# The first row of tokens turned ahead of the last projection quarter, and the next stage's first products of that row begun early

## The chip, the cores and the metric

The kernel runs on one core of one Trainium2 chip. Its engines are TensorE (PE; its weight loads, which overlap the products, are shown as PEld), VectorE (DVE), ScalarE (ACT), GpSimd (POOL) and SyncE (SP), which issues the transfers. The metric is the device time of one execution in microseconds (us).

## The reference

A sequence of 256 tokens of width 1024 goes through two blocks. The first has an attention layer with two kinds of heads (causal attention and differential attention) and a feed-forward layer that chooses 16 of 16384 experts for each of 8 heads. The second has two more attention layers, mixer A (three dilated groups) and mixer B (a neighbourhood on a grid). Everything is float32. Cut to what matters here:

```python
h = rms_norm(x, attn_norm); proj = h @ w_in          # attention of block 1 on proj
x = x + mixed @ w_out                                # the output projection
h = rms_norm(x, ffn_norm)                            # peer_ffn
q = (h @ w_query).reshape(C, 8, 2, 128)              # the first thing it computes
sc = einsum('thpd,hpnd->thpn', q, sub_keys)          # top 16, experts, gelu, sum
x = x + peer_out
hn = rms_norm(x, norm_gain[0]); x = x + mixer_a(hn)  # ends in y @ w_out, too
hn = rms_norm(x, norm_gain[1]); x = x + mixer_b(hn)  # starts with hn @ w_in
```

At each `rms_norm` all 1024 values of a token's x must be there, and the product behind it needs the normed tokens with the width on the partitions: they are turned (transposed) by TensorE.

## The kernel before, in words

x lies in on-chip memory as two rows of 128 tokens (`NT` = 2), each 1024 wide. The width is also cut into `KD` = 8 steps of 128, over which TensorE sums a product.

`attention_phase` runs three times: `block1` (named `block` in the trace), `mix_a` and `mix_b`. Each has one instruction list per engine, written in order: an engine works its list in order and waits at semaphores. A phase is a `Block`, at whose end all engines meet; the next phase starts on all of them together. Its pairs of heads go through a written schedule (`times_of`, `due`, `step`): products of the normed tokens with a weight piece into the banks `pj[0]` and `pj[1]`, eviction, norm of queries and keys, their turn (`turn_qk`), scores, softmax, turn, product with the values (`ot`), turn of the output (`yp`).

The output projection has four quarters b: row b // 2 of tokens, half b % 2 of the width, eight steps k each (`project`, line 720). Their banks are `acc`: `pj[0]`, `pj[1]`, `xp` and the first half of `sc`. A few of these steps are set between the last attention steps (`in_tail`); the others follow at the end in the order of `at_end`, line 503: first quarter 0, last quarter 3. In `block1` seven steps of quarter 3 are left at the end, k = 1 to 7; in `mix_a` all eight. A float32 product of this kind is two instructions in the trace.

Then comes the norm for the next phase (where `after` is given: `block1` and `mix_a`). VectorE adds a quarter to x (`add`); ScalarE squares a row and sums it; VectorE makes the root and scales the row (`next_scaled`, line 1098); TensorE turns it in eight transposes into two banks (line 775; row 0 into `pt` and the second half of `sc`, row 1 into `pj`); VectorE writes each half times the gain into `whole` (`next_window`, line 1104); ScalarE copies it, rounded, into `hT` high, and VectorE writes the rest into `hT` low (`next_low`, line 1110). In the lists before the change TensorE turns both rows after all four quarters, VectorE makes row 0's windows after the last addition and its low parts after the second row is scaled, and ScalarE squares both rows before it copies. Fillers (`keep_clock`, line 218: products with the unit matrix that nobody reads) stand between the two turns, behind the second, and at the start of `mix_b`; `WARM` has their numbers.

After `block1` the routing stage starts (`route_phase`). SP issues four loads of `route_raw` in the order 2, 3, 0, 1, then the first loads of the early chunks (each behind one of the first two query products), then reloads. TensorE makes 16 query products. The first two are plain, `down_raw` with `whole` over all 256 tokens (line 1422; their weights were loaded in the phase before). From the third on the weight is split: ScalarE writes the high part (line 1458), GpSimd the low part (line 1409), and TensorE makes three passes (lines 210 to 212). Behind each query product but the first stand the scores of the query before (line 1439), which also need that query's `route_raw`.

`mix_b` starts with the split of its first weight piece, `mix_raw` (ScalarE line 802, VectorE line 582), in four parts; the product of row 0 and that of row 1 run in three passes of 384 columns for each step, then the gate product in three passes of 256 (its weight, transferred from the start of the phase, is split at lines 881 and 1045), then the first product of the next pair, and behind its first part the turn of the first pair's queries and keys (line 667), which needs their norm from VectorE (lines 902 to 919).

Of the kernel before, what the change touches and what calls it, by code (L numbers as in the profile page):

```python
# [30 lines left out]
P = 128  # L31
# [37 lines left out]
WARM = {"open": 8, "row": 14, "last": 8, "experts": 10, "added": 10, "rows": (11, 6), "mix_b": 6}  # L69
# [245 lines left out]
def attention_phase(nc, name, pieces, *, n_pairs, kinds, groups, hT, yT, cons, q_gain=None, k_gain=None,  # L315
                    bias=None, load_bias=None, near=None, minus_lam=None, ahead=None, behind=None, finish=None, x, wo, wo_landed, fills, beside=None, lead=None, after=None, out=None):
# [88 lines left out]
    with ExitStack() as c:  # L405
# [48 lines left out]
        pj = [ps(f"pj{b}", [P, 512]) for b in range(2)]  # L454
# [3 lines left out]
        ot = ps("ot", [P, 2, SEQ])  # L458
        yp_bank = ps("yp", [P, 512])
# [37 lines left out]
        def pj_of(par, i):  # L497
            return (nch * par + i) % 2
# [8 lines left out]
        def _(sp):  # L507
# [20 lines left out]
            def one(q, qb):  # L528
# [6 lines left out]
                if ring == 1:  # L535
                    load_piece(q + 2, qb, 0)
# [59 lines left out]
        def _(pe):  # L596
# [10 lines left out]
            def product(q, qb, i, part):  # L607

                dst, j = pj[pj_of(qb, i)], piece_of[i]
                if lead is not None and isinstance(q, int) and q == 0 and i == NT and part == 0:  # L610
                    pe.wait_ge(first_low, 2 * NT)
# [40 lines left out]
                if part == cut - 1:  # L652
                    mm.then_inc(products, 1)

# [131 lines left out]
        def _(act):  # L786
# [103 lines left out]
            if after is not None:  # L890
# [3 lines left out]
                for n in range(2 * NT):  # L894
                    act.wait_ge(next_full, n + 1)
# [1107 lines left out]
```

## Time and profile before

| | us |
|---|---|
| median of 3 runs | 1597.7 |
| lowest, highest | 1596.82, 1598.11 |
| the profiled execution | 1597.93 |
| its span, from the first to the last instruction | 1596.2 |
| TensorE busy | 1549.2 |
| VectorE busy | 1012.3 |
| ScalarE busy | 690.8 |

A line of a timeline has the start in us from the span's start, the duration in us, the engine, the line of the kernel, the operation, what it writes and reads, its shape and how many like it were merged; in square brackets the time that the engine had been idle before it and who released it. "SPq" is the queue of transfers that SP issues. A line of a windows view has the stretch, its length, the busy time and number of instructions of each engine, the granted clock of TensorE (1.00 is 2.4 GHz), the share of time that the DMA engines were busy, and GB/s.

### The profile page before, as it was taken

The page shows a single profiled execution, that of the slowest core. Times are in us where ns is not written, and L with a number is a line of the kernel's source. Part 1 is how long each engine was busy: PE and PEld are TensorE (multiplying, and loading weights), DVE is VectorE, ACT ScalarE, POOL GpSimd, SP SyncE. Part 2 cuts the span into 40 slices and gives each one's busy share as a digit, 9 for nine tenths or more (in the row PEclk, how much of TensorE's full clock was granted, in tenths as well). Part 3 has the DMA queues.
Part 4 walks back from the last instruction along what each step waited for, and adds up shares of the span by engine and source line. Part 5 has one row for each costly group of instructions (what it writes and reads, how often), then busy time and mean ns, then how long its engine had stood idle before and what let it go on. Part 6 is the DMA issues. An engine that isn't in the chain of part 4 may idle for free. (4 is left out here: it accounts for less than half of the span.)

```text
span 1596.2 us, 29115 instructions
## 1 busy us (share of the span) xinstructions
PE 1549.2 (97%) x9001; PEld 1351.8 (85%) x9001; DVE 1012.3 (63%) x2525; ACT 690.8 (43%) x1537; POOL 42.0 (3%) x42
## 2 busy tenths in 40 slices
PE   7998999999999999999999999999999999899998
PEld 4664698888888888999999999979999999669994
DVE  4666589967776776666666666665555555247762
ACT  2433241222223444444444444435666655336661
POOL 0000160000000000000000000000000000000000
PEclk9999999999999999999999999999999999999999
DMA  7410344433225555655555555547544443317530
GB/s 285 169 56 1 119 145 144 152 100 93 93 80 197 191 191 178 204 184 184 186 186 190 186 189 189 186 161 230 178 146 146 145 147 120 116 30 230 160 110 27
DMA packets 163803, 240.40 MB, mean 151 GB/s; under 512 B 41744, under 2 KB 91408, under 8 KB 162192
## 3 DMA queue, kind: packets, MB, share of 16 engines
q1 hardware_dynamic: 163728, 239.46, 46.5%
q8 instruction: 39, 0.64, 0.2%
q14 instruction: 36, 0.29, 0.1%
HBM read 238.14 MB, written 1.29 MB: 150 GB/s over the span
## 5 line engine op out<-in xcount | busy, mean ns | idle before, releaser
L210 PE MATMUL experts_acc<-experts_uh,experts_wh 128*128 128x512 f32 x512 | 200.3, 391 | 0.4 <-DVE experts_ul L1787 0.4
L211 PE MATMUL experts_acc<-experts_ul,experts_wh 128*128 128x512 f32 x512 | 200.1, 391 | 0.0
L212 PE MATMUL experts_acc<-experts_uh,experts_wl 128*128 128x512 f32 x512 | 199.2, 389 | 0.0
L1257 PE MATMUL plain_u<-whole,down_raw 128*128 128x256 f32 x832 | 190.6, 380 | 0.7 <-PEq L1342 0.4
L1757 ACT ACTIVATE experts_uh<-whole 128x512 fp32r<-128x512 f32 x256 | 147.0, 623 | 81.0 <-PE experts_acc L212 75.4
L212 PE MATMUL projection<-hT_high,down_low 128*128 128x256 f32 x608 | 172.1, 283 | 0.0
L211 PE MATMUL projection<-hT_low,down_high 128*128 128x256 f32 x608 | 172.0, 283 | 0.0
L210 PE MATMUL projection<-hT_high,down_high 128*128 128x256 f32 x608 | 171.7, 282 | 0.0
L1257 PEld LDWEIGHTS plain_u<-whole,down_raw 128*128 128x128 f32 x832 | 152.5, 190 | 20.1 <-issue 1.7
L1787 DVE TENSOR_TENSOR experts_ul<-whole,experts_uh 128x512 fp32r<-128x512 f32 x256 | 164.7, 684 | 0.0
L210 PE MATMUL mix_a_pj<-mix_a_wh,hT_high 128*128 128x384 f32 x368 | 129.1, 351 | 0.0
L212 PE MATMUL mix_a_pj<-mix_a_wh,hT_low 128*128 128x384 f32 x368 | 123.5, 336 | 0.0
L211 PE MATMUL mix_a_pj<-mix_a_wl,hT_high 128*128 128x384 f32 x368 | 123.5, 336 | 0.0
L1793 DVE TENSOR_TENSOR experts_full<-experts_full,spread 128x256 f32<-128x256 f32 x76 | 32.3, 425 | 141.3 <-ACT experts_full L1322 141.3
L210 PEld LDWEIGHTS projection<-hT_high,down_high 128*128 128x128 f32 x608 | 116.4, 191 | 2.9
L211 PEld LDWEIGHTS projection<-hT_low,down_high 128*128 128x128 f32 x608 | 116.4, 191 | 2.9
L212 PEld LDWEIGHTS projection<-hT_high,down_low 128*128 128x128 f32 x608 | 116.4, 191 | 0.0
L1298 ACT ACTIVATE down_high<-down_raw 128x512 fp32r<-128x512 f32 x152 | 95.3, 632 | 46.5 <-DMA down_raw<-in_downT 41.3
L212 PEld LDWEIGHTS experts_acc<-experts_uh,experts_wl 128*128 128x128 f32 x512 | 96.2, 188 | 20.5
L210 PEld LDWEIGHTS experts_acc<-experts_uh,experts_wh 128*128 128x128 f32 x512 | 96.4, 188 | 18.8 <-issue 0.8
L211 PEld LDWEIGHTS experts_acc<-experts_ul,experts_wh 128*128 128x128 f32 x512 | 96.4, 188 | 17.1
L1322 ACT ACTIVATE experts_full<-projection 128x256 f32<-128x256 f32 x76 | 29.2, 384 | 178.9 <-PE projection L212 178.9
(362 smaller groups left out, 3065.7 us busy)
## 6 DMA issues: line engine op xcount, KB each, us to landing
down_raw<-in_downT SPq DMA_DIRECT2D x256, 256.0 KB, 3.4
whole<-in_up SPq DMA_DIRECT2D x256, 256.0 KB, 2.9
mix_raw<-in_wa SPq DMA_DIRECT2D x46, 768.0 KB, 6.1
block_w_raw<-in_w SPq DMA_DIRECT2D x16, 768.0 KB, 6.3
mix_raw<-in_wb SPq DMA_DIRECT2D x16, 768.0 KB, 7.4
route_raw<-in_route SPq DMA_DIRECT2D x16, 576.0 KB, 4.0
wo<-in_wo SPq DMA_DIRECT2D x4, 1024.0 KB, 8.3
mix_a_w_gate<-in_wa SPq DMA_DIRECT2D x8, 512.0 KB, 7.9
```

The source lines that it names most:

```text
L210: pe.matmul(out, lhs[0], rhs[0], start=start, stop=False, skip_group_check=True)
L211: pe.matmul(out, lhs[0], rhs[1], start=False, stop=False, skip_group_check=True)
L212: return pe.matmul(out, lhs[1], rhs[0], start=False, stop=stop, skip_group_check=True)
L1257: mm = pe.matmul(self.u[b][:, 0:SEQ], self.raw[b][:, k, :], self.h[:, k, :], start=k == 0, stop=k == KD - 1, skip_group_check=True)
L1298: act.activation(self.high[b][:, self.half(h)], self.raw[b][:, self.half(h)], ACT.Copy).then_inc(self.highs, 1)
L1322: act.activation(into, self.u[b][:, 0:SEQ], ACT.Gelu).then_inc(self.done, 1)
L1757: act.activation(uh[b][:, w], raw_u[b][:, w], ACT.Copy).then_inc(u_high, 1)
L1787: dve.tensor_tensor(ul[b][:, w], raw_u[b][:, w], uh[b][:, w].bitcast(F32), ALU.subtract).then_inc(u_low, 1)
L1793: dve.tensor_tensor(full[:], full[:], spread[:, n - READY, :], ALU.mult)
```

## The change

On TensorE, the turn of row 0 (`turn_next(0)`) moves in front of the first step of quarter 3 in `at_end`. Behind the quarters, a function `follow` of the next stage runs, then fewer fillers, then the turn of row 1. In `block1`, `follow` makes both plain query products for the tokens of row 0; the routing stage then makes them for row 1 only. In `mix_a`, `follow` makes steps 0 to 5 of `mix_b`'s first product, as a plain product with the unsplit weight; `mix_b` adds steps 6 and 7 in the same way instead of the eight steps in three passes. SP waits in `mix_b` for this first product before it loads over its weight. The banks of `ot` and `yp` in `block1`, and of `ot` in `mix_a`, are handed to the next stage and hold these products. VectorE makes row 0's windows and low parts ahead of the last addition; ScalarE copies row 0 ahead of the square of row 1. The fillers between the turns go from 14 to 4 (`block1`) and 0 (`mix_a`), those behind the second turn from 8 to 6, and the 6 at the start of `mix_b` are left out.

```diff
-WARM = {"open": 8, "row": 14, "last": 8, "experts": 10, "added": 10, "rows": (11, 6), "mix_b": 6}
+WARM = {"open": 8, "row_block1": 4, "row_mix_a": 0, "last": 6, "experts": 10, "added": 10, "rows": (11, 6), "mix_b": 6}
...
+                    if begun is not None and isinstance(q, int) and q == 0:
+                        sp.wait_ge(products, 1)
                     load_piece(q + 2, qb, 0)
...
+                if begun is not None and isinstance(q, int) and q == 0 and i == 0:
+                    if part == cut - 1:
+                        for k in range(per_part * part, KD):
+                            mm = pe.matmul(dst[:, 0:3 * P], begun["full"][:, k, 0:P], pieces.raw[0][:, k, :], start=False,
+                                           stop=k == KD - 1, skip_group_check=True)
+                        mm.then_inc(products, 1)
+                    return
...
-            if out is not None:
-                keep_clock(pe, yp[:, 0:P], ident[:], WARM[name])
             in_steps(pe, step)
             for k, b in at_end:
+                if after is not None and b == 3 and (k, b) == min(v for v in at_end if v[1] == 3):
+                    pe.wait_ge(pts_ready, before(n_pairs))
+                    pe.wait_ge(biased, before(n_pairs))
+                    turn_next(0)
                 project(k, b)
             if after is not None:
-                for t in range(NT):
-                    if t == 0:
-                        pe.wait_ge(pts_ready, before(n_pairs))
-                        pe.wait_ge(biased, before(n_pairs))
-                    else:
-                        keep_clock(pe, yp[:, 0:P], ident[:], WARM["row"])
-                    pe.wait_ge(next_h_ready, t + 1)
-                    for k in range(KD):
-                        mm = pe.transpose(turned_banks[2 * t + k // 4][:, k % 4, :], next_h[:, t, k * P:(k + 1) * P], ident[:])
-                        if k % 4 == 3:
-                            mm.then_inc(next_turned, 1)
-                keep_clock(pe, yp[:, 0:P], ident[:], WARM["last"])
+                follow(pe, next_full)
+                keep_clock(pe, pt[:, 0:P], ident[:], WARM["row_" + name])
+                turn_next(1)
+                keep_clock(pe, pt[:, 0:P], ident[:], WARM["last"])
...
                     act.activation(next_h[:, t, :], x[:, t, :], ACT.Square, accum_out=next_sum[:, t:t + 1]).then_inc(next_summed, 1)
-                for n in range(2 * NT):
-                    act.wait_ge(next_full, n + 1)
-                    act.activation(window(after["hT"][0], n), window(after["full"], n), ACT.Copy).then_inc(next_high, 1)
+                    for n in (2 * t, 2 * t + 1):
+                        act.wait_ge(next_full, n + 1)
+                        act.activation(window(after["hT"][0], n), window(after["full"], n), ACT.Copy).then_inc(next_high, 1)
...
             add(2)
-            add(3)
             if after is not None:
                 next_window(0)
                 next_window(1)
-                next_scaled(1)
                 next_low(0)
                 next_low(1)
+            add(3)
+            if after is not None:
+                next_scaled(1)
                 next_window(2)
...
                     if first:
-                        mm = pe.matmul(qp[b % 2][:, 0:SEQ], ahead.raw[b][:, k, :], ahead.h[:, k, :], start=k == 0, stop=k == KD - 1,
+                        mm = pe.matmul(ahead.u[b][:, P:SEQ], ahead.raw[b][:, k, :], ahead.h[:, k, P:SEQ], start=k == 0, stop=k == KD - 1,
                                        skip_group_check=True)
...
+            def first_queries(pe, full):
+                for b in range(2):
+                    pe.wait_ge(first_landed[b], 16)
+                    for k in range(KD):
+                        if b == 0 and k % 4 == 0:
+                            pe.wait_ge(full, k // 4 + 1)
+                        pe.matmul(plain_u[b][:, 0:P], down_raw[b][:, k, :], whole[:, k, 0:P], start=k == 0, stop=k == KD - 1,
+                                  skip_group_check=True)
...
+            def first_product(pe, full):
+                for k in range(KD - 2):
+                    if k % 4 == 0:
+                        pe.wait_ge(full, k // 4 + 1)
+                        pe.wait_ge(pieces_b.landed[0][k // 4], 16)
+                    pe.matmul(handed[:, 0:3 * P], whole[:, k, 0:P], raw[0][:, k, :], start=k == 0, stop=False, skip_group_check=True)
```

`turn_next(t)`, not shown, is the loop over eight transposes for row t, as it stands in the lines taken out.

## Rows read from the trace of the kernel before

**Rows 1.** The page: busy time of each engine; granted clock in 40 slices.

```profile
PE 1549.2 (97%) x9001; PEld 1351.8 (85%) x9001; DVE 1012.3 (63%) x2525; ACT 690.8 (43%) x1537; POOL 42.0 (3%) x42
...
PEclk9999999999999999999999999999999999999999
```

**Rows 2.** Timeline, 167 to 183 us: start, duration, engine, line, what, [idle, releaser].

```profile
167.75 6.17 PE L734 MATMUL block_sc<-wo,yT 128*128 128x512 f32 x14
...
170.61 0.75 DVE L1102 TENSOR_SCALAR block_next_h<-x,block_next_r 128x1024 f32<-128x1024 f32 x1
...
173.76 0.60 PE L775 MATMUL block_pt<-ident,block_next_h 128*128 128x128 f32 x4
...
173.96 0.69 DVE L1096 TENSOR_TENSOR x<-x,block_sc 128x512 f32<-128x512 f32 x1 [2.00 <-PE block_sc L734]
...
174.57 0.68 DVE L1107 TENSOR_TENSOR whole<-block_pt,columns 128x512 f32<-128x512 f32 x1
...
174.64 3.29 PE L218 MATMUL block_yp<-ident 128*128 128x128 f32 x28
...
178.69 1.28 DVE L1112 TENSOR_TENSOR hT_low<-whole,hT_high 128x512 fp32r<-128x512 f32 x2
...
178.83 1.09 PE L775 MATMUL block_pj<-ident,block_next_h 128*128 128x128 f32 x8 [0.90 <-DVE block_next_h L1102]
...
179.89 1.28 DVE L1107 TENSOR_TENSOR whole<-block_pj,columns 128x512 f32<-128x512 f32 x2
...
181.27 1.29 DVE L1112 TENSOR_TENSOR hT_low<-whole,hT_high 128x512 fp32r<-128x512 f32 x2
```

**Rows 3.** Timeline, 182 to 191 us, the start of the routing stage.

```profile
182.82 2.59 SPq L1391 DMA_DIRECT2D route_raw<-in_route  x4
...
182.87 7.14 PE L1422 MATMUL route_qp<-whole,down_raw 128*128 128x256 f32 x32 [1.16 <-PEq L405]
...
187.51 1.15 ACT L1458 ACTIVATE route_w_high<-route_raw 128x512 fp32r<-128x512 f32 x2 [0.53 <-DMA route_raw<-in_route]
...
188.22 2.49 POOL L1409 TENSOR_TENSOR route_w_low<-route_raw,route_w_high 128x512 fp32r<-128x512 f32 x2 [171.67 <-ACT route_w_high L1458]
...
190.93 0.36 PE L210 MATMUL route_qp<-hT_high,route_w_high 128*128 128x256 f32 x1
```

**Rows 4.** Timeline, 197 us, GpSimd's split of the fifth query weight.

```profile
197.04 2.51 POOL L1409 TENSOR_TENSOR route_w_low<-route_raw,route_w_high 128x512 fp32r<-128x512 f32 x2 [3.48 <-ACT route_w_high L1458]
```

**Rows 5.** Timeline, 1411 to 1420 us, the end of mixer A.

```profile
1411.35 0.75 DVE L1102 TENSOR_SCALAR mix_a_qT<-x,mix_a_next_r 128x1024 f32<-128x1024 f32 x1
...
1413.09 7.03 PE L734 MATMUL mix_a_sc<-woa,yT 128*128 128x512 f32 x16
```

**Rows 6.** Timeline, 1431 to 1445 us, the start of mixer B.

```profile
1431.30 0.44 PE L210 MATMUL mix_b_pj<-mix_b_wh,hT_high 128*128 128x384 f32 x1 [0.29 <-DVE mix_b_wl L582]
...
1434.27 1.07 ACT L881 ACTIVATE mix_b_gh<-mix_b_w_gate 128x1024 fp32r<-128x1024 f32 x1 [1.80 <-DMA mix_b_w_gate<-in_wb]
...
1435.37 1.29 DVE L1045 TENSOR_TENSOR mix_b_gl<-mix_b_w_gate,mix_b_gh 128x512 fp32r<-128x512 f32 x2 [1.51 <-ACT mix_b_gh L881]
...
1439.74 0.28 PE L210 MATMUL mix_b_pj<-hT_high,mix_b_gh 128*128 128x256 f32 x1
...
1440.63 0.69 DVE L902 TENSOR_REDUCE mix_b_ssum<-mix_b_sq 128x8 f32<-128x512 f32 x1 [1.58 <-ACT mix_b_qk L820]
...
1444.07 0.69 DVE L919 TENSOR_TENSOR mix_b_qk<-mix_b_qk,mix_b_root 128x512 f32<-128x512 f32 x1
...
1444.82 0.66 PE L667 MATMUL mix_b_xp<-ident,mix_b_qk 128*128 128x128 f32 x4 [1.05 <-DVE mix_b_qk L919]
```

**Rows 7.** Waits of TensorE, and windows with its granted clock, in mixer A's tail.

```profile
PE mix_a_pj L734 <- DMA woa<-in_woa: 4.5, 1, 4.5
...
1376.00:1378.00 2.00, 1.87 (x6) 1.15 (x6) 1.57 (x4) 0.00 (x0) 0.00 (x0) 0.67 1.06 398
...
1378.00:1380.00 2.00, 2.00 (x7) 1.49 (x7) 0.42 (x1) 0.00 (x0) 0.00 (x0) 0.50 1.06 373
```

More of the change, by code:

```diff
@@ L315, in attention_phase @@
 def attention_phase(nc, name, pieces, *, n_pairs, kinds, groups, hT, yT, cons, q_gain=None, k_gain=None,
-                    bias=None, load_bias=None, near=None, minus_lam=None, ahead=None, behind=None, finish=None, x, wo, wo_landed, fills, beside=None, lead=None, after=None, out=None):
+                    bias=None, load_bias=None, near=None, minus_lam=None, ahead=None, behind=None, finish=None, x, wo, wo_landed, fills, beside=None, lead=None, after=None, banks=(), follow=None, begun=None,
+                    out=None):
     roped = kinds[0] != "bias"
@@ L453, in attention_phase @@
             second = sb("second", [P, SEQ])
-        pj = [ps(f"pj{b}", [P, 512]) for b in range(2)]
+        banks = dict(banks)
+        pj = [banks["pj"] if b == 0 and "pj" in banks else ps(f"pj{b}", [P, 512]) for b in range(2)]
         xp = ps("xp", [P, NT, 2, P])
@@ L1234, with __init__ @@
 class Ahead:
[L1238 to L1240 removed]
+    def __init__(self, nc, ctx, u, down, hT, h, raw):
+        self.u, self.down, self.hT, self.h, self.raw = u, down, hT, h, raw
         self.landed = [[ctx.enter_context(nc.semaphore(f"plain_landed{b}_{h}")) for h in range(2)] for b in range(2)]
@@ L1464, in one @@
                 wait(act, s_ready, hp - 1)
-                act.activation(qh[b % 2][:], qp[b % 2][:, 0:SEQ], ACT.Copy).then_inc(q_kept, 1)
+                steps_in = ahead.u[b] if isinstance(hp, int) and hp < 2 else qp[b % 2]
+                act.activation(qh[b % 2][:], steps_in[:, 0:SEQ], ACT.Copy).then_inc(q_kept, 1)
             steps(act, one)
@@ L1908, in build @@
                                 cons=sbt, minus_lam=sbt["minus_lam"][:], ahead=store_pad, beside={"vector": scales, "scalar": shifted_rows}, behind=load_wo, finish=finish_first, x=x, wo=wo,
-                                wo_landed=landed, fills=FILLS_1, after={"gain": column("ffn", KD), "full": whole, "hT": hT})
+                                wo_landed=landed, fills=FILLS_1, after={"gain": column("ffn", KD), "full": whole, "hT": hT},
+                                banks={"ot": plain_u[0], "yp": plain_u[1]}, follow=first_queries)
             with ExitStack() as c:
-                c1 = c.enter_context(ExitStack())
                 slots = c1.enter_context(nc.psum_tensor("slots", [P, 4, SEQ], F32))
-                ahead = Ahead(nc, c, c1, d["downT"], hT, whole, down_raw)
+                ahead = Ahead(nc, c, plain_u, d["downT"], hT, whole, down_raw)
                 early = sb("early", [P, READY, SEQ], c=c)
@@ L1970, in build @@
                                 finish=load_pieces_b, x=x, wo=wo, wo_landed=landed, fills=FILLS_A,
-                                after={"gain": column("mix_b", KD), "full": whole, "hT": hT})
+                                after={"gain": column("mix_b", KD), "full": whole, "hT": hT}, banks={"ot": handed}, follow=first_product)
             with ExitStack() as c:
@@ L1986, in build @@
                                 q_gain=column("q_b", 1), k_gain=column("k_b", 1), bias=bias, load_bias=load_b,
-                                near=sbt["near"], ahead=lambda sp: pieces_b.load_gate(sp, 0), behind=load_wo, x=x, wo=wo, wo_landed=landed, fills=FILLS_B, out=out)
+                                near=sbt["near"], ahead=lambda sp: pieces_b.load_gate(sp, 0), behind=load_wo, x=x, wo=wo, wo_landed=landed, fills=FILLS_B, out=out, banks={"pj": handed},
+                                begun={"full": whole})
 def kernel(**inputs):
```

16 lines of the change are left out of this document (11 added, 5 removed).

## The prediction

> **What bounds the kernel now.** I read the page first, for the engine that has no slack. TensorE is busy for 97% of the span at the full granted clock, VectorE for 63% [rows 1]. The change touches TensorE's work at two places only, the handover from the first attention block to the routing stage (about 167 to 191 us) and the handover from mixer A to mixer B (about 1411 to 1445 us). So the second view was the timeline of all engines over these two stretches. What counts there is which chain carries the end of each stage, since behind it TensorE runs nearly without a pause and a shift of its start reaches the end of the kernel undiminished.
>
> The first handover shows that chain plainly [rows 2]. The last projection quarter runs on TensorE from 167.75 for 6.17 us. Its end lets the addition into x begin (173.96), then comes the norm of the second row of tokens, its turn on TensorE (178.83), two windows (179.89), their low parts, the last of which ends at 182.56, and then the new stage starts on TensorE at 182.87 [rows 3]. Everything between the quarter's end and 182.87 hangs on the quarter's end. Meanwhile the first row was ready to be turned at 170.61 + 0.75 = 171.36, in the middle of the quarter, and was turned only at 173.76. In mixer A the last quarter is longer, 16 instructions and 7.03 us from 1413.09, and its first row is ready at 1411.35 + 0.75 = 1412.10, ahead of the quarter [rows 5].
>
> **The change, part by part.** Times are those of the profiled execution: 1597.93 us with a span of 1596.2, so 1.7 lie around it; it stands 0.2 above the median of 1597.7. I sum shifts and add them to the median.
>
> *The turn ahead of the quarter, first handover.* In the first block seven of the eight products of the last quarter stand after the turn now, and TensorE reaches the turn at about 167.8, where the quarter's products started before. The first row is ready at 171.36. TensorE works in order, so the whole quarter waits behind this wait: 3.6 us of nothing. Then come eight transposes; before, the fillers behind them started 174.64 − 173.76 = 0.88 after the first. The quarter starts at 171.36 + 0.06 (the distance from the scaled row to the turn that the second row shows) + 0.88 = 172.3 in place of 167.75: **+4.6 us**, and the addition into x with it. The first row's windows, copies and low parts are now made while the quarter runs, which it covers: they need about 0.68 × 2 and 1.28 and end before 175, while the quarter ends at 178.5.
>
> *What the chain behind the quarter gets back.* In the kernel before, VectorE makes the first row's low parts (178.69, 1.28 us) between the second norm and the second row's windows, so the windows start at 179.89, which is 1.06 after the transposes begin. With nothing in between they start as the first row's did, 174.57 − 173.76 = 0.81 after the transposes begin [rows 2]. **−0.25**. ScalarE's square of the second row no longer stands near the copies of the first, but it had never waited for them: no price. The stage end thus shifts by +4.4 and the routing stage starts at about 187.2.
>
> *The first row's query products.* 32 instructions of 128 columns run in the time of the second norm. The nearest row is the filler, 28 instructions of that shape in 3.29 us, 0.1175 each, so 3.8 us from 178.5 to 182.3; with 8 fillers (0.9) TensorE is free at 183.2, and the second row, turned at 178.83 before, is ready at 178.83 + 4.6 = 183.4. The products are hidden. Fillers (28 cut to 8, 16 to 12) cost nothing for the same reason; if the row came earlier, at most the 0.9 would show. In the routing stage the same 32 instructions on 128 columns replace 32 on 256 that took 7.14: again 3.8, so TensorE is 3.4 us earlier with them.
>
> *What this is worth there.* The next work of TensorE is the scores and the third query, and the third query needs GpSimd's split [rows 3]. Counted from the stage's start (182.82): the first weight lands just before ScalarE takes it at +4.7, GpSimd starts at +5.4 and has the first half at +6.65. Before, the third query started at 190.93, +8.1. So at most 1.45 of the 3.4 can be had. Ahead of it stand the scores of the first query, which need the third weight transfer; its landing isn't shown, only that it was there at +7.6, where they ran. Bounds for the gain: 0 (it lands at +7.6) and 1.45 (before +6.2). The four transfers are issued one after another within 2.59 us, and the loads for the early chunks, which wait for the query products, now follow sooner and compete more. One more place limits it: the fifth query weight was reloaded after the first scores, and its split began at 197.04 after 3.48 us of idle GpSimd [rows 4], so this reload also ends no earlier than the scores move. I take 0.9, between the ends. First handover: 4.4 − 0.9 = **+3.5** (bounds +2.95 and +4.4). Nothing in the routing stage takes it back, since the shift is common to all engines.
>
> *The turn ahead of the quarter, second handover.* The row is ready 1.0 us before TensorE gets to the quarter [rows 5], so only the transposes are put in: +0.9. The chain behind gets back the same 0.25. The stage end shifts by **+0.7**. Six of the eight steps of mixer B's first product run in the gap of the norm: 12 instructions of 384 columns, by 7.14/32 for 256 columns 0.335 each, 4.0 us; the row's turn comes 4.9 us after the quarter, if it goes as at the first handover (178.83 against 173.92): hidden.
>
> *What mixer B gains.* Before, the first product took from 1431.30 half of the 48 instructions up to the gate product at 1439.74, 4.22 us, and was paced by the weights' split [rows 6]. Now the second product waits for that split, at 1431.3 + 0.7 = 1432.0, instead of starting at 1435.5. The two left steps (4 instructions, 1.3 us) fit in front of it. TensorE is 3.5 earlier, and the second product ends at 1436.2. The gate product then needs VectorE's low half of the gate weights. ScalarE took those when their transfer landed (1434.27, issued at the stage's start, so now 1435.0), VectorE follows with its first half at 1436.7: 0.6 lost, 2.9 left, gate from 1436.8. Then comes the turn of the first pair's queries and keys. It already waited 1.05 us for VectorE's norm (1444.82) [rows 6]. That norm starts with the sum at 1440.63, which had waited 1.58 for ScalarE. VectorE can be there 1.58 earlier at best, and since the gate transfer, and with it VectorE's earlier work, is 0.7 later, it starts 0.9 to 1.0 earlier. The chain up to the end of 1444.07 + 0.69 is unchanged in length. TensorE reached this turn at 1444.82 − 1.05 = 1443.77, 4.0 after the gate's start, so it arrives at 1440.8 now, waits 3 us and is only **0.95** ahead of before. Bounds: 0.3 (ScalarE's gate copy then runs into its copy of the turned keys) and 2.9 (the norm doesn't bind). I take 0.95, whose terms all have a row.
>
> SP's new wait for the first product stands before the loads of mixer B's third piece; that product ends at about 1431.5, and the low parts that the same load awaits end two microseconds later, so nothing is queued behind it for longer. The banks handed over cost nothing by themselves.
>
> Sum: +3.5 − 0.95 = +2.55. The forecast is 1597.7 + 2.55 = **1600.3 us**; its own range is 1599.2 to 1601.6.
>
> **The clock.** TensorE fell to the lower level after its one long pause in the middle of the kernel: 4.5 us waiting for the output weights, then a granted clock of 0.67 and 0.50 in the next two stretches of 2 us, which is the 1.2 GHz level for most of them, against 1.00 at 2.4 GHz elsewhere [rows 1, 7]. That cost 2 × 0.33 + 2 × 0.5 = 1.7 us. The changed kernel has three new pauses on the path: 3.6 us before the turn, about 3 before the first scores, 3 before mixer B's turn. The pauses of 0.9 to 1.2 us in [rows 2, 3, 6] passed at the full clock, so these lie between. The Trainium skill (TensorE: Matmul & The Clock Gate, HAM oscillation — how this bites in real kernels) says that a TensorE that waits between bursts is throttled again and starts each next burst cold; by that rule each new pause would be paid twice. The trace agrees for 4.5 us and is silent about 3.
>
> **The rivals.**
> 1. *The clock falls in the new pauses*, and the work behind each runs at half rate for a while. For it: the pause of 4.5 us. Against: they are shorter. Price 1.7 each, deciding once the pause is long enough for a fall: 1600.3 + 1.7 = 1602.0 with one, 1603.7 with two, 1605.4 with three. Slower for certain. 31%.
> 2. *The norm at mixer B doesn't bind*, because ScalarE or VectorE take their work in another order than I read, and 2.9 is kept: 1600.3 − 1.95 = 1598.3. Against: TensorE already waited there. 12%.
> 3. *Both new stages are bound by TensorE alone*, and all prepared work is kept: +4.4 − 3.4 at the first handover, −3.5 at the second, −2.5 together, 1595.2. Against: the split at +6.65. 7%.
> 4. *The wait in front of the turn isn't there*, the first row being ready when TensorE gets to it: then only 0.9 of the 4.6 is paid there and the sum is 2.55 − 3.7 = −1.15, 1596.5. Against: 171.36 stands in the rows, and nothing in the change moves that norm. 3%.
>
> The forecast has 47%.
>
> **How the numbers follow.** About 0.2%, 3.2 us, is what a measurement of this kernel can tell from no change: 1594.5 to 1600.9. Slower by more: all of rival 1 (31) and the upper fourth of the forecast's own range (11), 42%. Faster by more: no case reaches it with its likeliest value; 6% for the lower edge of rivals 3 and 4 and for what I have not seen. The rest, 52%, is within. The range of 8 in 10 leaves out rivals 3 and 4 and the case of three falls: 1598.0 to 1604.0.
>
> **What would show it.** Right: TensorE idle for 3.6 us before the turn, from about 167.9, released by VectorE's scaled row; the last addition of the first block at about 178.6; the routing stage's first product at about 187.2 and its third query 7 to 8 us after that; mixer B's second product at 1432 plus the shift, and a wait of 3 us before its first turn, released by VectorE. Wrong: a quarter that starts before 171; a third query more than 8.1 us or less than 6.6 after the stage's start; a turn in mixer B without a wait. A granted clock of 0.5 behind one of the pauses speaks for rival 1.

## The result and the profile after

The changed kernel takes **1603.2 us** (median of 6 runs, 1602.09 to 1604.77) against 1597.95 of the kernel before on the same chip (6 runs, 1596.82 to 1598.37): ratio **1.0035, interval [1.0023, 1.0047]**. It is slower. The forecast was 1600.3; the case that came about is rival 1 with two falls of the clock, for which the prediction had 1603.7. The profiled execution took 1602.87 us with a span of 1601.1. Of all executions timed for this document one, of the last kernel, ran in a slow state (1735.0 us at a mean granted clock of 0.85), and its ratio leaves it out.

The page of the changed kernel, its first lines, shows nearly nothing of that: TensorE is busy 3.4 us less than in [rows 1], the span is 4.9 longer.

```profile
span 1601.1 us, 29031 instructions
...
PE 1545.8 (97%) x8957; PEld 1345.7 (84%) x8957; DVE 1013.5 (63%) x2525; ACT 691.2 (43%) x1537; POOL 41.9 (3%) x42
```

The timeline of the changed kernel over the first handover (start, duration, engine, line, what, idle and releaser) answers to [rows 2 and 3]:

```profile
170.61 0.75 DVE L1114 TENSOR_SCALAR block_next_h<-x,block_next_r 128x1024 f32<-128x1024 f32 x1
...
171.51 0.84 PE L669 MATMUL block_pt<-ident,block_next_h 128*128 128x128 f32 x4 [3.61 <-DVE block_next_h L1114]
...
173.00 7.27 PE L752 MATMUL block_sc<-wo,yT 128*128 128x512 f32 x14
...
180.10 3.73 PE L1876 MATMUL plain_u<-whole,down_raw 128*128 128x128 f32 x32
...
180.30 0.69 DVE L1108 TENSOR_TENSOR x<-x,block_sc 128x512 f32<-128x512 f32 x1 [4.98 <-PE block_sc L752]
...
185.17 1.09 PE L669 MATMUL block_pj<-ident,block_next_h 128*128 128x128 f32 x8 [0.44 <-DVE block_next_h L1114]
...
188.85 3.81 PE L1434 MATMUL plain_u<-whole,down_raw 128*128 128x128 f32 x32 [1.25 <-PEq L406]
...
193.76 1.15 ACT L1470 ACTIVATE route_w_high<-route_raw 128x512 fp32r<-128x512 f32 x2 [2.47 <-DMA route_raw<-in_route]
...
196.69 1.19 PE L1451 MATMUL route_sp<-route_raw,route_qh 128*128 128x128 f32 x4 [4.03 <-DMA route_raw<-in_route]
...
197.53 0.56 PE L210 MATMUL route_qp<-hT_high,route_w_high 128*128 128x256 f32 x1
```

TensorE waits 3.61 us for VectorE's scaled row. Behind it the four transposes take 0.84 and the quarter 7.27 us, where the same forms took 0.60 and 6.17 in [rows 2]. At the start of routing it waits again, 4.03 us, this time for a weight transfer, and the four products behind that take 1.19 (0.68 where the clock is full, below). The windows of the changed kernel over these two places (stretch, its length, busy time and count of PE, PEld, DVE, ACT, POOL, then the granted clock, DMA share, GB/s) give the reason:

```profile
169.00:171.00 2.00, 0.00 (x0) 0.00 (x0) 1.53 (x7) 0.00 (x0) 0.00 (x0) 1.00 0.01 4
171.00:173.00 2.00, 1.49 (x9) 1.52 (x9) 1.57 (x3) 0.00 (x0) 0.00 (x0) 0.69 0.00 0
173.00:175.00 2.00, 2.00 (x4) 0.97 (x4) 1.74 (x4) 1.26 (x2) 0.00 (x0) 0.50 0.00 0
175.00:177.00 2.00, 2.00 (x5) 0.81 (x5) 0.32 (x1) 0.00 (x0) 0.00 (x0) 0.95 0.00 0
...
193.00:195.00 2.00, 0.00 (x0) 0.00 (x0) 0.00 (x0) 1.24 (x3) 0.53 (x1) 1.00 1.01 410
194.00:196.00 2.00, 0.00 (x0) 0.00 (x0) 0.00 (x0) 2.00 (x5) 1.53 (x2) 0.92 1.01 411
196.00:198.00 2.00, 1.31 (x6) 1.34 (x7) 0.08 (x1) 0.29 (x1) 2.00 (x2) 0.50 1.02 394
198.00:200.00 2.00, 2.00 (x11) 2.00 (x11) 1.84 (x12) 0.00 (x0) 1.42 (x2) 0.50 0.90 267
200.00:202.00 2.00, 2.00 (x12) 2.00 (x11) 0.85 (x6) 0.00 (x0) 0.00 (x0) 0.50 0.53 208
202.00:204.00 2.00, 2.00 (x17) 2.00 (x17) 0.61 (x4) 1.12 (x3) 0.14 (x1) 0.88 0.00 0
```

A granted clock of 0.50 is the 1.2 GHz level. It comes with each of the two pauses, as in [rows 7] with the one of 4.5 us. The two falls are not equally long. By the shares in these windows the first lasts some 3.4 us (0.69, 0.50 and 0.95 in three stretches of 2 us). The second begins before TensorE resumes (0.92 in 194 to 196), stays at 0.50 up to 202 and makes 6.8 us, of which TensorE works for 5.8. The Trainium skill (TensorE: Matmul & The Clock Gate, HAM oscillation — how this bites in real kernels) says that bursts with waits between them each start cold; this trace agrees behind its waits of 3.61 and 4.03 us, where the granted clock is 0.69 and 0.50 in the first window of work.

The timeline of the changed kernel at the second handover answers to [rows 5 and 6]:

```profile
1427.36 4.03 PE L1970 MATMUL handed<-mix_raw,whole 128*128 128x384 f32 x12
...
1427.56 0.69 DVE L1108 TENSOR_TENSOR x<-x,mix_a_sc 128x512 f32<-128x512 f32 x1 [4.46 <-PE mix_a_sc L752]
...
1432.79 1.09 PE L669 MATMUL mix_a_pj<-ident,mix_a_qT 128*128 128x128 f32 x8 [1.39 <-DVE mix_a_qT L1114]
...
1438.34 0.44 PE L210 MATMUL mix_b_pj<-mix_b_wh,hT_high 128*128 128x384 f32 x1 [0.34 <-DVE mix_b_wl L586]
...
1440.96 1.06 ACT L893 ACTIVATE mix_b_gh<-mix_b_w_gate 128x1024 fp32r<-128x1024 f32 x1 [1.46 <-DMA mix_b_w_gate<-in_wb]
...
1442.05 1.29 DVE L1057 TENSOR_TENSOR mix_b_gl<-mix_b_w_gate,mix_b_gh 128x512 fp32r<-128x512 f32 x2 [1.16 <-ACT mix_b_gh L893]
...
1445.65 0.68 DVE L914 TENSOR_REDUCE mix_b_ssum<-mix_b_sq 128x8 f32<-128x512 f32 x1
...
1449.85 0.66 PE L685 MATMUL mix_b_xp<-ident,mix_b_qk 128*128 128x128 f32 x4 [2.21 <-DVE mix_b_qk L931]
```

From mixer A's last addition (1427.56) to the turn of the first pair it is 22.3 us now and was 24.7 (1420.16 to 1444.82). The turn waits 2.21 for VectorE, which is now without the 1.58 us of idle ahead of the sum, and which also starts on the gate weights nearer behind the last addition: 1442.05 − 1427.56 = 14.5 against 15.2.

**The account**, by how much later the same instruction stands than in the trace before (each step is the difference of two rounded shifts):

| place | before | after | later by | step |
|---|---|---|---|---|
| last addition, first block | 173.96 | 180.30 | 6.3 | +6.3 |
| routing starts | 182.87 | 188.85 | 6.0 | −0.3 |
| first scores | 190.49 | 196.69 | 6.2 | +0.2 |
| third query | 190.93 | 197.53 | 6.6 | +0.4 |
| early chunks (first product behind routing) | 239.0 | 247.0 | 8.0 | +1.4 |
| experts start | 489.4 | 495.7 | 6.3 | −1.7 |
| last addition, mixer A | 1420.16 | 1427.56 | 7.4 | +1.1 |
| turn of mixer B's first pair | 1444.82 | 1449.85 | 5.0 | −2.4 |
| last addition of all | 1592.40 | 1597.35 | 5.0 | 0 |

The second fall accounts for most of the +0.4 and +1.4: from the scores to the early chunks it was 48.5 us before (190.49 to 239.01) and is 50.3 now (196.69 to 246.98). At half the rate over 5.8 us of work it would be 2.9 by itself; 1.8 shows.

The −1.7 at the experts is no gain of the change. The 10 fillers there (20 instructions) follow the same pause of 1.58 us in both kernels; in the trace before the clock fell behind it and after it did not. First the kernel before, its timeline and a window, then the timeline of the kernel after:

```profile
485.51 4.10 PE L218 MATMUL projection<-ident 128*128 128x128 f32 x20 [1.58 <-PEq L1574]
...
486.00:488.00 2.00, 2.00 (x12) 2.00 (x11) 1.93 (x5) 1.68 (x4) 0.00 (x0) 0.50 0.75 234
```

```profile
493.50 2.47 PE L218 MATMUL projection<-ident 128*128 128x128 f32 x20 [1.58 <-PEq L1587]
```

### The profile page after: what moved, and what is told of

Its sections match the earlier page's. It is cut to its first block and busy times, and to the rows that moved or that the text cites. A ratio compares the mean times of both kernels' runs of the same rounds, so it can differ in the third digit from the quotient of the medians.

```text
span 1601.1 us, 29031 instructions
## 1 busy us (share of the span) xinstructions
PE 1545.8 (97%) x8957; PEld 1345.7 (84%) x8957; DVE 1013.5 (63%) x2525; ACT 691.2 (43%) x1537; POOL 41.9 (3%) x42
```

## The experiments

**Theory**: at the first handover the turn makes the whole quarter wait (+4.6), each of the two pauses of about 4 us costs a fall of the clock (1.7), the prepared query products give nothing back, since the first scores wait for a weight transfer; at the second handover 1.5 are won. **Rivals**: the prepared products do give back; the price is in the changed bookkeeping and not in the clock; the second handover wins nothing. All ratios are to the kernel before, timed on the same chip (its median was 1598.67 for the kernels of experiments 1 to 3, 1597.61 for those of 4 to 6, 1598.15 for the two of 7). They are the recorded ones and differ by up to 0.0003 from the quotient of the two medians. The diffs show the lines that matter, with each experiment's values written in; in the kernels they hang on a table of options, `OPT`.

**1. The second handover alone, and the first alone.** Each puts the other handover back as it was: turn, fillers, windows and copies in the order of before.

```diff
+            early = name in ("mix_a",)     # the first: ("block1",)
             for k, b in at_end:
-                if after is not None and b == 3 and (k, b) == first_of_quarter:
+                if after is not None and early and b == 3 and (k, b) == first_of_quarter:
                     turn_next(0)
                 project(k, b)
+            if after is not None and not early:
+                turn_next(0)
+                keep_clock(pe, yp[:, 0:P], ident[:], 14)
+                turn_next(1)
+                keep_clock(pe, yp[:, 0:P], ident[:], 8)
```

> The change at the second handover alone (mixer A to mixer B); the first block and the routing stage as before. Theory: the loss of the whole change comes from the first handover, and the second one gains. Between the traces of before and after, the shift goes from +6.5 us at mixer A's first addition to +5.0 at mixer B's first turn, so alone it should give 1597.9 - 1.5 = 1596.4 us. Rival: the second handover gives nothing by itself and only hides a part of a late start; then 1597.9, or above it if its +0.9 of transposes shows. Between 1595.8 and 1597.0 the theory holds; from 1597.7 up the rival.

> The change at the first handover alone (first block to routing stage); mixer A and mixer B as before. Theory: +4.6 for the quarter behind its wait, +1.7 for the clock's fall behind it, about +1 to +2 more in the routing stage, where TensorE waits 4 us for the scores' weights and falls to the lower clock again: 1603.9 to 1606.0 us, and with the second handover's part the two sum to the whole change (1603.2). Rival: the loss is a matter of both parts together, or of clock falls that have nothing to do with the pauses: then under 1602.5.

Second alone: 1597.42 us, 0.9995 [0.9986, 1.0004]. First alone: 1604.11, 1.0033 [1.0021, 1.0046]. The whole loss is the first handover's. The gain of the second is in the trace: 22.6 us from mixer A's last addition to the turn, 24.7 before, less the 0.9 of transposes ahead of that addition. The time stands 1.2 us below that of before by the medians and 0.8 by the ratio, whose interval holds 1, so by time the gain isn't shown. Nor is it shown by the last addition of all (1591.2, 1.2 ahead of before), since this trace has no fall at 485 us and a longer one in mixer A (experiment 7).

**2. The clock at the first pause.** 14 fillers on finished data run in the pause, ahead of the wait for the row. Nothing else is changed.

```diff
                     pe.wait_ge(biased, before(n_pairs))
+                    keep_clock(pe, pt[:, 0:P], ident[:], 14)   # block1 only
                     turn_next(0)
```

> The whole change, with 14 fillers (28 instructions, 3.3 us by before's row) in front of the first row's turn in the first block, in the pause of 3.6 us. The wait for the row stays, only TensorE isn't idle in it. Theory (the pause costs its length and, by the clock's fall, 1.7 us more): 1603.2 - 1.7 = 1601.5 us, and the granted clock behind the turn is 1.00. Rival (the clock falls there for another reason, or the fall costs nothing since something else is late): 1603.2. If the fillers were late themselves, up to 1603.5.

1601.08 us, 1.0015 [1.0006, 1.0024]. Its timeline:

```profile
171.38 0.66 PE L670 MATMUL block_pt<-ident,block_next_h 128*128 128x128 f32 x4 [0.38 <-DVE block_next_h L1134]
...
172.31 6.17 PE L753 MATMUL block_sc<-wo,yT 128*128 128x512 f32 x14
...
194.32 1.19 PE L1481 MATMUL route_sp<-route_raw,route_qh 128*128 128x128 f32 x4 [3.46 <-DMA route_raw<-in_route]
```

The turn still comes at 171.4, but the quarter is back to 6.17 us and the last addition stands at 178.52, 4.56 later than before: the 4.6 of the prediction, with nothing on top. The changed kernel has 6.34, so the unfilled pause costs 1.78 more there (0.13 of it ahead of the turn, at 171.51 instead of 171.38). By the ratios, each taken on its own chip, the two kernels are 0.0020 apart, which is 3 us, with intervals that just overlap; in the traces the ends are only 0.3 apart (1597.01, 1597.35), since this profile has another fall, at 1448 to 1453 behind mixer B's pause. That one cost 1.74: from mixer B's first turn to the last addition of all it is 149.24 us here (1447.77 to 1597.01) and 147.50 in the changed kernel. The fall at the wait for the weight transfer (3.46) is there too.

**3. The wait itself.** The turn is put inside the quarter, behind 8 of its 14 instructions, where TensorE stands when the row gets ready.

```diff
-                if after is not None and b == 3 and (k, b) == first_of_quarter:
+                if after is not None and (k, b) == (5 if name == "block1" else 0, 3):
```

> The whole change, but in the first block the first row is turned inside the last quarter, behind its step 4 and in front of step 5 instead of in front of step 1: four steps of 0.86 us fill the time until the row is ready at 171.4. Theory: no pause, no fall of the clock there, the quarter ends 0.9 later than before instead of 6.3: 1603.2 - 5.4 = 1597.8 us, and with the second handover's gain no slower than before. Rival (the halved query products, the earlier loads and the pause before the first scores make the loss): it stays above 1601.

1599.49 us, 1.0006 [0.9997, 1.0015]. Its timeline:

```profile
171.41 0.63 PE L670 MATMUL block_pt<-ident,block_next_h 128*128 128x128 f32 x4 [0.17 <-DVE block_next_h L1134]
...
172.31 2.74 PE L753 MATMUL block_sc<-wo,yT 128*128 128x512 f32 x6
...
183.63 3.81 PE L1462 MATMUL plain_u<-whole,down_raw 128*128 128x128 f32 x32 [1.25 <-PEq L407]
...
191.60 0.68 PE L1481 MATMUL route_sp<-route_raw,route_qh 128*128 128x128 f32 x4 [4.17 <-DMA route_raw<-in_route]
```

The 3.6 us are gone and routing starts at 183.63, 0.8 behind before. There the prepared products should show: they free TensorE 3.3 us earlier, at 187.4. The scores come at 191.60, 7.97 behind the start; before it was 7.62. TensorE stands for 4.17 us, and nothing is given back. (The profiled run is the fastest of its 11, 1596.79. Its mean granted clock is 0.998 and that of the others 0.995 to 0.997, so the trace shows less of the falls than the median holds.)

**4. Are the prepared query products worth anything?** The turn stays inside the quarter, the 32 products of the first row are left to the routing stage again, and 18 fillers stand there instead of 4.

```diff
-                for b in range(2):
+                for b in ():              # no product of the first row ahead
...
-                        mm = pe.matmul(ahead.u[b][:, P:SEQ], ahead.raw[b][:, k, :], ahead.h[:, k, P:SEQ], ...)
+                        mm = pe.matmul(ahead.u[b][:, 0:SEQ], ahead.raw[b][:, k, :], ahead.h[:, k, 0:SEQ], ...)
```

> As the kernel with the turn inside the quarter, but the first row's query products are not made early: 18 fillers stand in their place, and the routing stage makes both products for both rows as in the kernel before. Theory: the prepared products bring nothing, since the scores wait for their weight's transfer anyway, and their only effect is a pause in which the clock falls; so without them the time is 0 to 1 us lower: 0.9995 to 1.0006 of before. Rival: they save a part of their 3.4 us, and without them the kernel is 1 to 3.4 us slower than 1.0006: 1.0012 to 1.0027.

1597.18 us, 0.9995 [0.9986, 1.0004]. Its timeline:

```profile
183.65 7.15 PE L1464 MATMUL plain_u<-whole,down_raw 128*128 128x256 f32 x32 [1.25 <-PEq L407]
...
191.49 0.68 PE L1483 MATMUL route_sp<-route_raw,route_qh 128*128 128x128 f32 x4 [0.69 <-DMA route_raw<-in_route]
```

The same start, 3.3 us more products in the stage, and the scores at 191.49 instead of 191.60. So the products are worth nothing here: what TensorE is early by, it waits, 4.17 against 0.69. And no fall follows the wait of 0.69, while the fall after 4.17 is in the trace of the experiment before this one (granted 0.60 and 0.55 from 192 to 196). There it lasts 3.4 us and costs less than its half: from the scores to the early chunks it is 49.20 us (191.60 to 240.80) and here 48.47 (191.49 to 239.96), 0.7 apart.

**5. The transfer that binds.** The scores need the third of four weight transfers. With the loads in another order it is the second; then with 12 fillers ahead of the scores as well.

```diff
-            for b in (2, 3, 0, 1):
+            for b in (2, 0, 3, 1):
...
+                if hp == 1:               # the second kernel only
+                    keep_clock(pe, qp[1][:, 0:P], ident[:], 12)
```

> As the kernel with the turn inside the quarter (which was at 1.0006 of before), and the four first loads of the routing stage issued in the order 2, 0, 3, 1 instead of 2, 3, 0, 1. Theory: in the routing stage TensorE waits for the transfer of the first scores' weight (4.2 us there, the scores at +8.0 us after the stage's start), and this wait eats what the prepared query products save; as the second transfer it lands 1 to 1.5 us earlier, the third query then starts at about +7.0, and the time falls by about 1.2 us, more if the clock no longer falls in the pause: 0.9995 of before. Rival: the wait is for bandwidth that all transfers share, so the order moves nothing; or the third query is bound by the split of its own weight: 1.0006 again.

> As the one with the changed order of loads, with 12 fillers (24 instructions, 2.8 us) behind the second query product, in the pause before the first scores. Theory: the clock no longer falls in this pause, which is worth what it cost there (1 to 1.7 us when it fell): 0.9990 of before, and granted clock 1.00 behind the pause. Rival: the pause is now short enough without them, and both kernels agree within 0.5 us.

1597.75 us, 1.0001 [0.9992, 1.0010], and 1598.04, 1.0002 [0.9993, 1.0011]. Timeline of the first:

```profile
183.80 3.81 PE L1464 MATMUL plain_u<-whole,down_raw 128*128 128x128 f32 x32 [1.24 <-PEq L407]
...
190.67 0.68 PE L1483 MATMUL route_sp<-route_raw,route_qh 128*128 128x128 f32 x4 [3.06 <-ACT route_qh L1510]
...
199.54 0.38 PE L211 MATMUL route_qp<-hT_high,route_w_high 128*128 128x256 f32 x1 [1.44 <-POOL route_w_low L1450]
```

The scores come 6.87 behind the start (7.30 in the second kernel), released by ScalarE's eviction and no longer by the transfer. With the old order the nine traces in which they wait for it have 7.26 to 8.21, so the transfer did bind. It brings little: the next wait is for GpSimd's split, 1.44 at 199.54, and the early chunks start 56.4 us behind the stage's start, where they stood 56.1 behind it before the change. Earlier scores or products don't shorten this stage, whose weights have to land and be split. The fillers change nothing that the time shows; the first profile had no fall at this place without them.

**6. The second handover taken further.** The second handover alone, and mixer B's first gate weight loaded at the end of mixer A (into mixer A's gate buffer, free by then) instead of at mixer B's start, since its landing set VectorE's start there.

```diff
             def load_pieces_b(sp):
                 pieces_b.load(sp, 0, 0, 0)
                 pieces_b.load(sp, 1, 1, 0)
+                pieces_b.load_gate(sp, 0)      # no longer the first load of mixer B
```

> The change at the second handover alone, and the first gate weight of mixer B loaded at the end of mixer A (into the buffer that mixer A's gate weights no longer use) instead of at mixer B's start. Theory: what bounds the gain in mixer B is VectorE's list ahead of the first norm, which starts with the low half of the gate weight and so with this transfer; without its wait VectorE is 1.1 us earlier at the norm and TensorE's wait before the first turn (2.2 us) falls by as much: 1.1 us less than the second handover alone (0.9995 of before), so 0.9988. Rival: the norm is bound by ScalarE's evictions or by the products themselves; then the wait stays above 2 us and the time at 0.9995.

1597.08 us, 0.9995 [0.9986, 1.0004]: by time the edit adds nothing to the second handover alone, where 0.9988 was expected. In the trace the turn stands 21.0 us behind mixer A's last addition (1441.2 − 1420.2; 24.7 before, 22.6 without this edit). Part of this is lost again at once, 1.1 us between the turn and the last addition of all (148.72 against 147.58 before), where ScalarE awaits a second gate weight for 3.88 us. The last addition of all stands at 1589.93, 2.5 ahead of before, but that trace is one of the four executions with a mean granted clock of 0.999, which took 1594.95 to 1595.44; the six at 0.997 took 1597.08 to 1598.00 and hold the median.

**7. The oldest fall.** Every kernel so far has the pause of 4.0 to 4.5 us ahead of the output weights of mixer A, and the fall behind it [rows 7]. 16 fillers (each two instructions of 128 columns, 0.235) run in it: once with both handovers in the order of before, once on top of experiment 6.

```diff
+                if (k, b) == (0, 0) and name == "mix_a":
+                    keep_clock(pe, acc[0][:, 0:P], ident[:], 16)
                 pe.wait_ge(wo_landed[k // 4], 32)
```

> The kernel before's order at both handovers, with only the 16 filler matmuls in the pause of 4.4 us ahead of the output weights. Theory (the clock's fall behind the pause costs 1.7 us of its own): 0.9990 of the kernel before, and the stage behind the pause at a granted clock of 1.0 from its first instruction. Rival (the price of a fall is not there, or moves to another place): 1.000, with a window of granted clock below 0.9 elsewhere within the next 100 us.

> The second handover alone (row prepared ahead of the last quarter of mixer A's projection), mixer B's first gate weight loaded at the end of mixer A, and 16 filler matmuls on prepared data placed in the pause of 4.4 us in which TensorE waits for the output weights at the end of the experts. The kernel before and the kernel after both show TensorE at 1.2 GHz right behind that pause. Theory (a pause of this length makes the clock fall, and the fall costs some 1.7 us beside the pause): 16 fillers of 0.235 us, 3.8 us, end inside the wait and no fall follows, so 1.7 us less than the version with the gate weight moved (0.9995 of before, its last addition 2.5 us ahead of before's): about 0.998 of the kernel before by time, 0.9974 by the traces' positions. It should be faster than both kernels. Rival (falls come at random in the run and one avoided is replaced by another, or the fillers hold up what follows): 0.9995 to 1.000.

The fillers alone: 1596.31 us, **0.9986 [0.9977, 0.9995]**. With experiment 6: **1594.04 us, 0.9973 [0.9963, 0.9982]**, 4.1 us under the kernel before and, by the two ratios, 0.6% under the changed one. Timeline and windows of the fillers alone:

```profile
1372.62 3.84 PE L219 MATMUL mix_a_pj<-ident 128*128 128x128 f32 x32 [0.48 <-ACT mix_a_vt L852]
...
1376.30 1.02 PE L757 MATMUL mix_a_pj<-woa,yT 128*128 128x512 f32 x2
```

```profile
1376.00:1378.00 2.00, 2.00 (x16) 1.52 (x14) 1.94 (x4) 0.00 (x0) 0.00 (x0) 1.00 1.06 400
1378.00:1380.00 2.00, 2.00 (x7) 1.00 (x7) 0.47 (x2) 0.00 (x0) 0.00 (x0) 1.00 1.07 378
```

The first product on the weights starts at 1376.30 (1376.13 before), the clock is full, and from there to mixer A's last addition (1418.60) it is 42.30 us, where the kernel before needs 1420.16 − 1376.13 = 44.03. The fall had cost 1.73. The same distance without and with fillers on top of experiment 6 is 44.91 (1375.27 to 1420.18) and 43.17 (1375.82 to 1418.99), 1.74. In the trace of the fillers alone no window below 0.9 follows up to the last addition of all: the price does not move elsewhere, and the theory holds against its rival.

The fall here is not always that short. In three traces it begins before TensorE resumes and lasts 6.8 us: those of the two kernels of experiment 1 and of experiment 4. One of them, the second handover alone:

```profile
1374.00:1376.00 2.00, 0.71 (x1) 0.50 (x2) 1.70 (x6) 0.00 (x0) 0.00 (x0) 0.50 0.99 374
1376.00:1378.00 2.00, 2.00 (x7) 1.21 (x6) 1.02 (x3) 0.00 (x0) 0.00 (x0) 0.50 1.06 388
1378.00:1380.00 2.00, 2.00 (x7) 1.48 (x7) 0.42 (x1) 0.00 (x0) 0.00 (x0) 0.50 1.07 376
1380.00:1382.00 2.00, 2.00 (x5) 0.76 (x5) 0.00 (x0) 0.00 (x0) 0.00 (x0) 0.85 1.05 371
```

The same distance there is 45.83 us (1375.29 to 1421.12), 2.7 over the 43.17 with fillers; in experiment 4 it is 2.3 over (1375.92 to 1421.42), and with the first handover alone 3.3 over the 42.30 (1380.52 to 1426.14).

The last kernel's profile does have one fall left, behind the pause of 1.9 us at mixer B's first turn (1440 to 1445); from the sum ahead of it to the last addition of all it is only 0.3 us longer (153.23) than without a fall (152.92, experiment 6); that waits behind it took up the rest is likely and not shown.

## Why the prediction was right, and where it was not

The sign of its sum was right and its range of 8 in 10, 1598.0 to 1604.0, held the time, near its upper end. But the case that it took as likeliest (47%) was not the one that came, nor was the likeliest of its three outcomes: within 0.2% had 52%, slower, which it is, 42%. That rival 1 with two falls (1603.7) comes within 0.5 us of the time is in part luck: routing gave back 0.9 less, the second handover won 0.5 more, and a fall of the kernel before is missing after.

- *The turn makes the quarter wait, +4.6*: right. The pause is 3.61, the transposes as priced, and with the clock held up the last addition shifts by 4.56.
- *The chain behind gets back 0.25*: right, 0.36 from the last addition to the routing start. The stage start would have shifted by 4.2 with a full clock (187.06 in experiment 2), 4.4 was forecast.
- *Routing gives back 0.9 of 3.4*: wrong, it gives back nothing. The step that failed is "its landing isn't shown, only that it was there at +7.6": I took the value between the ends though the nearest row, the scores at +7.6, was itself an end and the likely one. Measured +7.84 in the changed kernel, +7.97 with the turn inside the quarter, and +7.84 with no product prepared at all. Over all traces with this order and a wait for it, it is +7.26 to +8.21, so no single trace fixes it to better than a microsecond. Cost of the error 0.9 and the 0.2 to 0.4 by which the scores came later still. The third query came at +8.7 (197.53 − 188.85), past the 8.1 that the prediction had named as a sign of being wrong.
- *The clock*: wrong in the weight; the size is right for the first fall and right by luck for the second. Rival 1 had the mechanism and the places, and its price of 1.7 is what the fall of 3.4 us cost (1.78, and 1.73 in mixer A). The second fall was twice as long, and 1.8 of its 2.9 showed. I gave the rival 31% because the pauses were shorter than the one of 4.5 us in [rows 7], and because I read the clock as 1.00 everywhere else. That reading was wrong: the trace before has a second fall, behind the 1.58 us at 485 us, and a slice of the page of 40 us does not show one. Two of the three places fell (3.61 and 4.03). The third, 2.21 at mixer B's first turn, did not fall in this profile; a pause of about that length there did in three of eight others.
- *Fillers cut to 8 and 12, the query products themselves, the handed banks: no price*: nothing in the trace speaks against it. The products took 3.73 (3.8 forecast) and the second row was turned 0.44 after TensorE was ready for it.
- *Second handover, stage end +0.7, sum −0.95*: direction right, too small. Measured +0.9 from the first product on the output weights (1376.13 and 1382.67) to the last addition, then −2.4 up to the turn, together about −1.5. VectorE's sum lost its whole idle time, as forecast; I then subtracted 0.6 to 0.7 because the gate weights would land later by the whole shift of the stage. ScalarE took them 13.4 us behind the last addition, 0.7 nearer than before (14.1). As that addition is 0.9 later, about 0.15 of the deduction was left: the stage started 0.4 nearer behind the addition, and the weights were taken 4.54 us behind their issue, where it had been 4.89.

The sum with measured sizes: 4.6 − 0.4 at the first handover, +0.2 at the scores, 1.8 for each of the two falls, −1.5 at the second handover make +6.5. Against it stands the fall at 485 us that the trace before has and the one after has not (−1.6), which leaves +4.9, the difference of the spans. By time it is +5.3, or +5.6 by the ratio. Where the falls lie in executions without a profile isn't shown. Their mean granted clock is shown: 0.998 in 57 of the 82 executions of the kernel before, as in its profile. The last us of this account stays open.

## What to carry to other kernels

Work moved ahead on an engine that works in order must be ready by the time the engine gets there, or everything behind it waits too; put the moved step where its input is just ready, in the midst of the long run of products if need be. Before pricing work that a later stage is spared, find what that stage waits for first: here a weight transfer stood 4 us behind TensorE, and 3.4 us of spared products became 3.5 us of wait. And price each new pause of TensorE of several us twice, as the pause and as a fall of its clock (1.7 us here, up to 3.3 when the fall is long), or fill it with work on finished data: at the one place where it was tried alone that was worth 0.14%. Look for falls in windows of 2 us, since the 40 slices of the page read 9 in all twelve kernels, and compare two traces only after counting the falls in each.

## What was not expected of the hardware

- A fall of 3.4 us costs 1.78, 1.73, 1.74 and 1.74 us at three places of these kernels where dense work follows. At mixer A's output weights it lasted 6.8 us in three traces and cost 2.3 to 3.3. Behind the wait for the scores' weight the short fall cost 0.6 and 0.7, the long one 1.8 and 2.3 (scores to early chunks, against 48.5 without a fall), and at mixer B's first turn the short one cost 0.3 in the last kernel; the likely reason is that part of the work behind waits anyway. What decides between the short and the long fall isn't shown.
- Every unfilled pause of 3.46 to 4.5 us at these places has a fall with it, in all traces. The shorter ones are not decided by their length alone: one of 3.06 (experiment 5) had none, behind the same 1.58 us at 485 the clock fell in one trace of twelve (4.10 us for the 10 fillers, 2.47 in the others), and behind some 2 us at mixer B's first turn it fell in three traces of nine.
- The falls are a good part of the 3 to 4 us by which executions of one kernel differ: in experiment 6 the executions with a mean granted clock of 0.999 and of 0.997 are 1.6 us apart at the least, and in experiment 2 the two at 0.995 took 1602.5 and 1602.7 and the two at 0.998 took 1600.2 and 1600.5.
- Of four transfers issued together in the old order, ScalarE got the first 4.95 us behind the issue in the changed kernel, and the third let the scores start at 7.84; over the traces that is 7.26 to 8.21. Brought forward by one place it was there at 6.87 or before.
